# A hybrid attention and mixture-of-experts layer: GpSimd's order of scatters and gathers in a pass, and the place of the first tile's sums at the end

## What is computed

```
scores = sigmoid(t @ w_router)            # 64 experts in 8 groups, 8 chosen for each token
wts    = scores[top_e] / sum * 2.5
routed = sum over the 8 chosen experts e of  wts_e * (silu(t @ w_gate[e]) * (t @ w_up[e])) @ w_down[e]
shared = (silu(t @ w_sh_gate) * (t @ w_sh_up)) @ w_sh_down
x      = x + g_f * rmsnorm(routed + shared, g_post_ffn)
```

## Time and profile before

| | |
|---|---|
| median of three runs | 1007.27 us (1006.61 to 1007.97) |
| profiled execution, its own time | 1007.2 us |
| its span, first to last instruction | 1005.4 us |
| mean granted TensorE clock | 0.984 |
| PE busy | 938.9 us, 93% |
| DVE busy | 520.6 us, 52% |
| POOL busy | 462.3 us, 46% |
| ACT busy | 330.3 us, 33% |
| passes of the experts, PE | 372.6 to 980.1 us |
| fold, last sums and stores | 980.1 to 1005.4 us |

### The profile page before, as it was taken

How to read it: one execution, slowest core, us unless ns; L and a number is a source line. 1 busy time by engine, 2 the same in 40 slices (tenths; PEclk the granted TensorE clock), 3 DMA queues, 4 the chain that set the end, 5 groups by cost and what they waited for, 6 DMA issues and landing times. The chain is left out here.

```text
span 1005.4 us, 14543 instructions
## 1 busy us (share of the span) xinstructions
PE 938.9 (93%) x4307; PEld 405.4 (40%) x4308; DVE 520.6 (52%) x717; ACT 330.3 (33%) x591; POOL 462.3 (46%) x342
## 2 busy tenths in 40 slices
PE   3999999999999999999999989998999999989875
PEld 1644444677456543333333333332333333333322
DVE  1336779786267954444443444444444333444457
ACT  4212222576345412232232222332222233222322
POOL 0312432000000147666776775765776676766611
PEclk9999999999999999999999989998999999999978
DMA  9955442420325969999979999999999999999775
GB/s 371 355 206 209 168 178 94 187 119 1 139 83 199 388 241 354 397 398 389 395 287 404 408 398 388 402 395 378 407 361 358 382 366 379 365 368 349 214 290 154
DMA packets 68448, 299.69 MB, mean 298 GB/s; under 512 B 21518, under 2 KB 22514, under 8 KB 39361
## 3 DMA queue, kind: packets, MB, share of 16 engines
q1 hardware_dynamic: 41522, 261.16, 65.5%
q0 software_dynamic: 25840, 35.98, 13.6%
q10 hardware_dynamic: 1056, 2.18, 0.6%
HBM read 284.78 MB, written 62.91 MB: 346 GB/s over the span
## 5 line engine op out<-in xcount | busy, mean ns | idle before, releaser
L1274 PE MATMUL psum<-wring,xres 128*64 (+1 forms) x1664 | 373.8, 602 | 17.5 <-DVE wring L1754 16.1
L581 POOL DMA_INDIRECT xg<-h_rows,gidx x208 | 256.5, 1233 | 179.5 <-issue 92.7
L1758 DVE STREAM_TRANSPOSE xres<-xg 128x1024 f32<-128x1024 f32 x52 | 106.4, 2046 | 259.4 <-DMA xg<-h_rows,gidx 258.5
L1274 PEld LDWEIGHTS psum<-wring,xres 128*64 128x64 f32 x1664 | 120.7, 139 | 234.7 <-issue 234.6
L1286 PE MATMUL psum<-wring,rows 128*64 x416 | 189.7, 599 | 7.8 <-DVE rows L1792 6.9
L1286 PE MATMUL psum<-rows 128*64 128x512 f32 x416 | 189.7, 599 | 0.0
L893 ACT COPY xres<-psum 128x1024 f32<-128x1024 f32 x52 | 52.6, 1012 | 278.4 <-DMA expert_sums<-xres,sidx 238.9
L1754 DVE COPY wring<-wring 128x1536 f32 x104 | 123.0, 1224 | 16.1 <-SPq L465 14.6
L1286 PEld LDWEIGHTS psum<-wring,rows 128*64 128x64 f32 x416 | 57.4, 138 | 126.5 <-issue 126.5
L832 ACT COPY rows<-wring 128x1024 f32 x104 | 103.5, 1046 | 7.9 <-PE psum L1286 7.5
L591 POOL DMA_INDIRECT expert_sums<-xres,sidx x50 | 81.8, 1636 | 15.2 <-issue 15.2
(11 more groups left out here) (273 smaller groups left out, 919.8 us busy)
## 6 DMA issues: line engine op xcount, KB each, us to landing
wring<-in_w_e_gate SPq DMA_DIRECT2D x64, 1024.0 KB, 8.5
wring<-in_w_e_up SPq DMA_DIRECT2D x64, 1024.0 KB, 15.1
wring<-in_w_e_down SPq DMA_DIRECT2D x64, 1024.0 KB, 17.3
ring<-in_w_ada SPq DMA_DIRECT2D x20, 1024.0 KB, 5.2
wring<-expert_sums SPq DMA_DIRECT2D x8, 1024.0 KB, 11.7
ring<-in_w_in SPq DMA_DIRECT2D x3, 2048.0 KB, 25.7
heads<-in_w_ada SPq DMA_DIRECT2D x4, 1024.0 KB, 23.3
ring<-in_w_out SPq DMA_DIRECT2D x1, 4096.0 KB, 12.7
```

Of the source, the lines that this page charges most:

```text
L581: pool.indirect_dma_start(xg[q][:, 256 * s:256 * s + 256], None, hrows, bass.IndirectOffsetOnAxis(gidx[:, q, s:s + 1].bitcast(U32), 0), bo ...
L1274: last = pe.matmul(pp[2][SUB * g:SUB * g + SUB, 512 * q:512 * q + 2 * F] .rearrange("p (u f) -> p u f", u=2), xT[:, q, k, SUB * g:SUB * g ...
L1758: dve.transpose(xT[:, q].rearrange("p k (s r) -> p s k r", s=4), xg[q].rearrange("p (s r k) -> p s k r", s=4, k=KD)).then_inc(s_xte, 1)
```

## The change

Two edits. In each pass POOL issues the scatter of p-2 ahead of the gather of p+2, in the two passes before the loop and in the loop. And DVE's `add_sums(0)` moves from inside the last iteration to behind it, so that `keep_hidden` of pass 51 stands ahead of it.

```
@@ gpsimd, before the loop @@
             for p in range(2):
+                scatter(p - 2, p, arow[:, 3], p + 1)
                 gather(p + 2, p, p + 2)
-                scatter(p - 2, p, arow[:, 3], p + 1)
@@ gpsimd, the loop over passes @@
                 for q in range(2):
+                    scatter(i + (q - 2), q, ysb[:, q], i + (q + 1))
                     gather(i + (q + 2), q, i + (q + 2))
-                    scatter(i + (q - 2), q, ysb[:, q], i + (q + 1))
@@ vector, the last iterations @@
-                if k == -1:
-                    add_sums(0)
                 if k != -3:
                     keep_hidden(q, passes(NT + 2 + k), passes(NT + 1 + k))
@@ vector, behind them @@
+            add_sums(0)
             add_sums(1)
```

## The result

| | before | after |
|---|---|---|
| median, nine runs of each on one chip | 1007.97 us (1006.02 to 1011.39) | 1015.35 us (1009.7 to 1020.21) |
| ratio, 95% interval | | 1.0053 [1.0033, 1.0073] |
| profiled execution, its span | 1007.2, 1005.4 us | 1009.7, 1007.8 us |
| mean granted TensorE clock | 0.984 | 0.986 |

The change made the kernel slower by about half a per cent. 999.0 us was forecast, and the time lies above the whole range. The profiled execution is the fastest of after's nine, so the +2.4 us between the two profiles is the low end of the loss.

What follows compares the result with a forecast made beforehand. The scatter's cycle, acting through the gather, was taken to bound passes 29 to 49. Terms: -8.0 (those passes) + 0.9 (last scatter) - 1.1 (sums) = -8.2 from 1007.2, so 999.0 us; range 996 to 1007, likeliest 996 to 1002.5.

Steps and rivals of the forecast that it cites:

- What bounds the kernel: Passes 29 to 49: the scatter's cycle takes 23.0 us for two passes, acting through the gather; 13.4 us lost there.
- The scatter's step: POOL's scatter starts at about T + 2.0 and lands at T + 14.6; slack 6.9 us, `keep_y`'s waits nearly gone.
- The gather starts at T + 5.2: POOL's gather, now behind the scatter, starts 5.2 us after `keep_y` starts, 1.25 us later than before.
- I lean to the first, the only row with the new spacing, and take 11.0: Late passes: 13.08 us from scatter's issue end to turning chosen over 15.03 and 14.55; 11.0 us a pass, 8.0 us gained.
- The first rival: Gather can't land before the scatter ahead: 11.47 us a pass, 229.4 us for passes 29 to 49, 1007.5 us; chance 0.13.
- the second rival: Gather lands 15.0 us or more behind the scatter's issue: 11.7 us a pass, 234 us, 1012 us in all; chance 0.12.
- The divisor: Late passes: the gather's chain, 4.9 + landing + 3.48 us, was taken to span two passes; slower from 14.4 us on.
- Before pass 29 little is to be had: Passes before 29: DVE's five waits, 14.6 us, were for weights, late in any POOL order; no change counted there.
- The last scatter and the weights' bound: Kernel's end: last scatter lands under the weight stream, +0.9 us; weights keep pass 50 from starting before about 934.
- the third rival: DMA engines are full, so loads slip as passes run ahead; pass 50 starts only 4 us early: 1003 us; chance 0.15.
- Edit 2, -1.1: Kernel's end: moving `add_sums(0)` behind the last `keep_hidden` gains 1.1 us, between nothing and 1.5.
- The 996 us at the range's foot: Lower end of the forecast range: 10.75 us a pass would give -13, but the weights allow about 10.

Runs made afterwards that it cites:

- e5: Against before: gather's indices set on ACT ahead of `keep_y`, POOL's old order, first sums moved as in the change; 1002.24 us, ratio 0.9934.
- e12: Against before: gather's indices set on ACT ahead of `keep_y`, POOL's old order, sums in their old place; 1001.93 us, ratio 0.9949.
- e1_order: Against before: only POOL's order changed, scatter ahead of gather, sums in their old place; 1013.56 us, ratio 1.0050.
- e6_gap: Against before: changed POOL order, old place of the sums, and POOL waits for PE's gate and up before it gathers; 1017.92 us, ratio 1.0101.
- e10_early_only: Against before: loop split in two, scatter ahead of gather only up to pass 29, sums in their old place; 1012.90 us, ratio 1.0052.
- e9: Against before: loop split in two, scatter ahead of gather only from pass 30 on, sums in their old place; 1016.07 us, ratio 1.0072.

## Why the prediction was wrong

In the profile -8.2 us was forecast and +2.4 measured. Two terms make up this miss of 10.6: the pace of 11.0 us for passes 29 to 49, which was 11.3 (6.7 us), and the nothing that was put at the passes before them (4.6 us). Both are the price of the later gather, which was priced too low in the one and left out in the other.

- **What bounds the kernel**, the scatter's cycle of 23.0 us for two passes: right for the old order. The 13.4 us lost there were to be had, 9 to 11 of them by e5 and e12 (7 to 11 against all profiles of the old order).
- **The scatter's step**: right. Its first DMA started at T + 2.0, and the waits at L893 went.
- **The gather starts at T + 5.2**: nearly right, 5.47 in the late passes. Where POOL's L588 overlaps DVE's copy (L1754), as at 887.21, it takes 1.55 us instead of 1.02.
- **"I lean to the first, the only row with the new spacing, and take 11.0"**: this step failed. From the end of the scatter's issue to the turning it is 15.0 us, not 13.08. The row comes from an early pass, 16, where scatters land 9.1 to 9.3 us after their end (medians of before and e1_order, passes 4 to 15); in the late passes it is 9.7 and 10.5. Nor was it the only one at 0.30 us: the gather at 384.95 us, of pass 3, followed a scatter so too, before any pass had rows to scatter, and was turned 12.2 us after that scatter's end. I matched the row by its spacing, which e6_gap shows to matter little, and not by the stretch. The first rival had the mechanism of this stretch, the gather's wait in the place of the scatter's, and it was given 0.13. Its 229.4 us were measured as 226.7. Its whole time, 1007.5, was too low, since it too put nothing at the early passes; that the measured 1015.35 lies nearer the second rival's 1012 is luck, for the second's 234 us did not come.
- **The divisor** was wrong as well. I closed the gather's chain over two passes from T, the start of `keep_y`. T itself lies 10.64 us behind a start of PE, and the chain closes at the third start after it, so an overrun is shared by three. That is why 15.0 us gave 11.46 a pass and not the second rival's 11.7 (with its own 15.0: (10.64 + 4.9 + 15.0 + 3.48) / 3 = 11.34). The point from which it is slower than 11.4 lies at 15.2 us, not 14.4.
- **"Before pass 29 little is to be had"**: true, and beside the point, since there was something to lose. In passes 5 to 15 the turn came 4.65 us ahead of PE's start before (median; 3.48 is the least) and 3.60 after: the later gather used up the slack there. This term was put at nothing on the strength of DVE's waits for weights, and the slack of the gathers was not looked at. e10_early_only shows the loss, and the starts that a gather held in passes 3 to 13 give its size: 3.1 to 4.1 us, where the old order has 0.0 to 0.8.
- **The last scatter and the weights' bound**: not tested by the change, since the passes never ran ahead. In e5 and e12 they did, and weights held no pass from 30 to 49, which speaks against the third rival. The bound at pass 50 is borne out: e12's had to wait for weights and started at 931.96, near the 934 that I had worked out. (The 996 us at the range's foot leave out the 0.9 for the last scatter; with it they are 997.)
- **Edit 2, -1.1**: right in size by the profiles (1.0 to 1.3), not resolved in the times.

The size of the whole: -8.0 became -1.3, nothing became +4.6, the end became -1.8 (forecast -0.2) and the start +0.8: +2.4 in the profile instead of -8.2. The medians say +7. The further 5 us have no row in this profile. e1_order's profile, of a run of 1014.74 us, has pass 29 at 710.0 (706.5 in after, 701.0 in before): 2.7 of these 9.0 us lie ahead of pass 0, which the change doesn't reach, and 6.3 between pass 0 and 29. There weights' arrivals vary from profile to profile: the starts in passes 3 to 13 that waited for them cost 2.6 to 8.0 us in the profiles that have the old order there. So where the rest of the loss of the medians lies stays open. In the profiles the late passes are no slower in the changed order (11.3 to 11.5 us from pass 33 on, 11.4 to 11.6 in the old); e9's times leave that open.

## What to carry to other kernels

A read that follows a write on one queue was seen as landed only some us after the write; moving the write ahead frees its buffer sooner and makes the read later, and the longer of the two cycles sets the pace. Count a cycle from a start of the bounding engine to the next start that it reaches, over as many passes as that takes, and take its durations from rows of the same stretch. When both orders are late at something, look for the instruction that lets the queue start at all: here an index copy of 0.2 us, set earlier, gained 0.5%, which reordering did not.

## What the runs showed of the hardware

- A gather's last landing trails that of the scatter ahead on the same queue by 4.5 to 4.7 us (medians, late passes), for gaps of 0.3 to 2.2 us between their issues and scatter landings of 7.0 to 15.5 us; its first increments come up to 7.6 us ahead of it.
- The rows of the scatters cost some 32 us of the whole time, 18 of them in passes that waited for weights and 13 in passes that waited for gathers; the issues alone cost PE nothing (10.74 us a pass).
- POOL's DMA issues that overlap DVE's copies of 128x1536 f32 elements take longer: in before, gathers took 1.60 us (median of 67, at most 2.44) beside one and 1.03 (median of 122, at most 1.07) without. The Trainium skill, SBUF — State Buffer, section "SBUF: two separate sides", says that such a copy keeps GpSimd from writing descriptors; these times agree.
